# Down products in 64-column tiles, their sums over 128 rows, and coarser refills of four weight places

## What is computed

```python
def run_block(args):
    toks, wts, e = args
    xb = hf[toks]
    y = (jax.nn.silu(xb @ w_gate[e]) * (xb @ w_up[e])) @ w_down[e]
    return y * wts[:, None].astype(y.dtype)
...
out = jnp.zeros((N, D), h.dtype).at[slot_tok].add(ys.reshape(n_slots, D).astype(h.dtype))
```

## Time and profile before

| | |
|---|---|
| median of 3 runs | 1597.59 us (1597.54 to 1599.92) |
| profiled execution: its own time | 1597.35 us |
| profiled execution: span | 1595.5 us |
| PE busy over the span | 1570.9 us (98%) |
| DVE, ACT, POOL busy | 895.5, 192.5, 36.1 us |
| transfers | 374.70 MB, mean 235 GB/s |
| granted TensorE clock | 0.998 |
| chain that ended last | PE 88%, DMA 6%, SPq 3%, DVE 1% |

### The profile page before, as it was taken

How to read it: one execution, slowest core, us unless ns; L and a number is a source line. 1 busy time by engine, 2 the same in 40 slices (tenths; PEclk the granted TensorE clock), 3 DMA queues, 4 the chain that set the end, 5 groups by cost and what they waited for, 6 DMA issues and landing times.

```text
span 1595.5 us, 20636 instructions
## 1 busy us (share of the span) xinstructions
PE 1570.9 (98%) x8777; PEld 998.7 (63%) x8777; DVE 895.5 (56%) x1549; ACT 192.5 (12%) x311; POOL 36.1 (2%) x60
## 2 busy tenths in 40 slices
PE   8999999999999999999999999999999999999997
PEld 4866499974458564999744876899533333333332
DVE  5896676765559876676646676795432223121122
ACT  1321000000114110000001331410000000000001
POOL 1001000000010010000000000000000000000000
PEclk9999999999999999999999999999999999999999
DMA  6532545563534336355536333446999999999997
GB/s 212 205 106 106 177 149 164 169 215 107 211 96 171 106 106 210 120 160 180 189 106 237 131 107 132 159 161 256 424 383 427 426 426 429 427 426 427 427 422 302
DMA packets 129781, 374.70 MB, mean 235 GB/s; under 512 B 17220, under 2 KB 65672, under 8 KB 116632
## 3 DMA queue, kind: packets, MB, share of 16 engines
q1 hardware_dynamic: 118864, 370.62, 61.1%
q10 hardware_dynamic: 10824, 2.72, 0.8%
HBM read 372.28 MB, written 1.05 MB: 234 GB/s over the span
## 4 chain that ended last, share of the span: by engine, by line
PE 88%; DMA 6%; SPq 3%; DVE 1%; issue 0%; ACT 0%; POOL 0%; POOLq 0%; DVEq 0%
PE bank L892 16%; PE bank L1204 16%; PE bank L823 10%; PE bank L1648 10%; PE bank L835 6%; PE bank L1694 5%; PE bank L1457 4%; DMA weights<-in_w_down 4%; SPq L703 3%; DMA arena<-in_w_up 3%; PE bank L1407 3%; PE bank L1329 2%; PE bank L1187 2%; PE bank L1490 2%; PE bank L1339 2%; PE bank L843 2%
## 5 line engine op out<-in xcount | busy, mean ns | idle before, releaser
L823 PE MATMUL bank<-weights,turned_rows 128*128 128x512 f32 x384 | 169.6, 598 | 0.4 <-DVE turned_rows L2167 0.4
L3314 DVE TENSOR_TENSOR bc<-mix,bank 128x512 f32<-128x512 f32 x16 | 17.2, 1077 | 212.6 <-PE bank L1648 212.6
L892 PE MATMUL bank<-arena 128*128 128x512 f32 x296 | 133.2, 592 | 0.0
L823 PEld LDWEIGHTS bank<-weights,turned_rows 128*128 128x128 f32 x384 | 72.7, 192 | 86.5 <-issue 85.9
L1204 PE MATMUL bank<-arena 128*128 128x128 f32 x960 | 110.5, 275 | 0.0
L1204 PEld LDWEIGHTS bank<-arena 128*128 128x128 f32 x960 | 108.8, 192 | 0.0
L892 PEld LDWEIGHTS bank<-arena 128*128 128x128 f32 x296 | 56.0, 190 | 69.9 <-issue 67.9
L835 PE MATMUL bank<-turned_rows,weights 128*128 128x256 f32 x448 | 98.6, 380 | 0.0
L1648 PE MATMUL bank<-arena,mix 128*64 128x512 f32 x304 | 92.3, 595 | 1.1 <-DMA arena<-in_w_up 0.6
L835 PEld LDWEIGHTS bank<-turned_rows,weights 128*128 128x128 f32 x448 | 84.6, 190 | 12.1 <-issue 0.7
L1694 PE MATMUL bank<-arena,mix 128*32 128x512 f32 x512 | 86.3, 594 | 2.5 <-DMA weights<-in_w_down 1.4
(11 more groups left out here) (542 smaller groups left out, 2490.4 us busy)
## 6 DMA issues: line engine op xcount, KB each, us to landing
weights<-in_w_in SPq DMA_DIRECT2D x28, 2048.0 KB, 7.9
arena<-in_w_gate SPq DMA_DIRECT2D x13, 2048.0 KB, 22.7
arena<-in_w_up SPq DMA_DIRECT2D x12, 2048.0 KB, 34.0
weights<-in_w_ffn_gate SPq DMA_DIRECT2D x22, 1024.0 KB, 5.4
weights<-in_w_ffn_up SPq DMA_DIRECT2D x22, 1024.0 KB, 8.1
weights<-in_w_ffn_down SPq DMA_DIRECT2D x10, 2048.0 KB, 7.8
arena<-in_w_down SPq DMA_DIRECT2D x10, 2048.0 KB, 29.7
weights<-in_w_out SPq DMA_DIRECT2D x8, 2048.0 KB, 8.3
```

Source lines behind the costliest of these rows:

```text
L823: ins = mm(b[:, :], xT[:, k, t0 + P * t:t0 + P * t + P], w[:, k, :], start=(k == 0), stop=(k == KD - 1))
L892: ins = mm(b[:, :], lhs[:, j, :], rhs[:, j, :], start=(first and j == 0), stop=(last and j == pairs - 1))
```

## The change

Pairs 0 to 13 get wide forms of four steps; pairs 14 and 15 keep the old ones. `wide_down` issues two products per k and half, one for each expert, in 64-column tiles, and leaves the places ordered expert, row tile, place. Then the places of a row tile no longer lie in one half of the partitions. So `wide_sum_up` multiplies all 128 rows, with weights that are zero for the places of the other row tile; there is such a weight matrix for each row tile, hence `wide_pick_weights` (the same four small operations, into two 128 x 128 matrices that are cleared once), `wide_picks_turned` (two transposes) and `wide_picks_back` (a copy of 256 columns). Places 1, 2 and 3 are refilled in halves.

```diff
-REFILL_PARTS = (4, 4, 4, 4, 4, 4, 2, 2)
+REFILL_PARTS = (2, 2, 2, 2, 4, 4, 2, 2)
...
+            def wide_sum_up(n):
+
+                for half in range(2):
+                    pe.wait_ge(sem(f"y_ready{half}"), n + 1)
+                pe.wait_ge(sem("pickT_ready"), n + 1)
+                for half in range(2):
+                    for t in range(NT):
+                        mm(moe_bank[4 + 2 * t + half][:, :], wide_pickT[:, P * t:P * t + P], yE[:, 512 * half:512 * half + 512],
+                           start=(n == 0), stop=True, skip_group_check=True)
...
+            def wide_picks_turned(n):
+
+                pe.wait_ge(sem("pickw_ready"), n + 1)
+                for t in range(NT):
+                    ins = nc.tensor.transpose(moe_bank[1][:, P * t:P * t + P], wide_pickw_rows[t], ident[:, :])
+                ins.then_inc(sem("pickT_full"), 1)
+
+            def wide_down(w, half, k):
+
+                for e in range(2):
+                    at = TILE_COLS * e
+                    ins = mm(moe_bank[2 + half][at:at + TILE_COLS, :], hidT[:, k, at:at + TILE_COLS], w[e](2 * k + half),
+                             start=(k == 0), stop=(k == KE - 1), skip_group_check=True)
+                return ins
...
                 if n > 1:
-                    sum_up(n - 2, n == 2)
+                    wide_sum_up(n - 2)
                 expand(n, 2, 1, half_ready, all_ready).then_inc(sem("up_full"), 1)
...
-                rows_down(n_)
+                wide_rows_down(n_)
...
-                picks_turned(n_)
+                wide_picks_turned(n_)
                 next_rows(n_)
...
+            def wide_picks_back(n):
+
+                v.wait_ge(sem("pickT_full"), n + 1)
+                nc.vector.tensor_copy(wide_pickT, moe_bank[1][:, 0:NT * P]).then_inc(sem("pickT_ready"), 1)
...
-            pick_weights(0, 0, None)
+            nc.vector.memset(bc[:, 256:256 + NT * P], 0.0).then_inc(sem("dve_step"), 1)
+            step()
+            wide_pick_weights(0)
```

More of the change, by code:

```diff
@@ L410, in program @@
         pickw = pickw_rows.rearrange("p (t e j) -> p e t j", e=2, t=NT)
-        pickT = bc[:, 384:512]
+        wide_pickw_rows = [bc[:, 256 + P * t:256 + P * t + P] for t in range(NT)]
+        wide_pickw = [v.rearrange("p (e t j) -> p e t j", e=2, t=NT) for v in wide_pickw_rows]
+        wide_pickT = wrt.rearrange("p k n -> p (k n)")[:, 0:NT * P]
+        pickT = wide_pickT[:, 0:P]
         hidE = bc[:, NBC2:NBC2 + DE]
@@ L1699, in down_weights, with wide_rows_down @@
                 return [landed(n, 4 + e) for e in range(2)]
-            def rows_down(n):
+            def wide_rows_down(n):
                 w = down_weights(n)
-                if isinstance(n, int) and n == 0:
+                if n == 0:
                     for k in range(KE):
                         for half in range(2):
-                            ins = down(n, w, half, k)
+                            ins = wide_down(w, half, k)
                             if k == KE - 1:
@@ L1712, in rows_down @@
                     return
+                for half in range(2):
+                    for k in range(KE):
+                        ins = wide_down(w, half, k)
+                    ins.then_inc(sem("y_full"), 1)
+            def rows_down(n):
+                w = down_weights(n)
                 for half in range(2):
@@ L3293, in pick_weights, with wide_pick_weights @@
                 ins.then_inc(sem("pickw_ready"), 1)
+            def wide_pick_weights(n):
+                if n:
+                    v.wait_ge(sem("pickT_full"), n)
+                for t in range(NT):
+                    for e in range(2):
+                        r_ = rank[:, t, n * 2 + e:n * 2 + e + 1]
+                        g_ = gate[:, t, n * 2 + e:n * 2 + e + 1]
+                        ins = TS(wide_pickw[t][:, e, t, :], place, r_, g_, ALU.is_equal, ALU.mult)
+                ins.then_inc(sem("pickw_ready"), 1)
             def rows_in(n, xs=xsE[1]):
@@ L3350, in _ @@
                 hidden_back(i + 1, bank=2 if i == PAIRS - 3 else 0)
-                picks_back(i)
+                wide_picks_back(i)
                 if i < PAIRS - 4:
@@ L3355, in _ @@
                     rows_in(PAIRS - 1)
-                pick_weights(i + 1, i + 1, i + 1)
+                if i < PAIRS - 3:
+                    wide_pick_weights(i + 1)
+                else:
+                    pick_weights(i + 1, i + 1, i + 1)
                 if i % 2 and i + 4 < PAIRS:
```

## The result

| | before | after |
|---|---|---|
| median of 4 runs each | 1597.92 us | 1612.02 us (1611.34 to 1612.46) |
| ratio, 95% interval | | 1.0082 [1.0069, 1.0096] |
| profiled execution: span | 1595.5 us | 1610.4 us |
| chain that ended last | PE 88%, DMA 6%, SPq 3% | PE 98%, DMA 0% |

The change makes the kernel 14 us slower, 0.8%. The forecast was 1613.7 us. The spans of the two profiled executions differ by 14.9 us, the medians by 14.1.

A forecast was written before the change was run, and what follows sets the result against it. TensorE and transfers were taken as nearly level in the expert stage, TensorE bounding it after the change. Span 1595.5 + 22.7 (sums) + 0.1 (transpose) - 6.7 (waits) = 1611.6 us, with 1.85 and 0.24 added 1613.7 us; range 1607 to 1618.5.

The forecast's parts named there:

- What bounds the kernel: Expert stage: TensorE and transfers both look full; PE's 6.7 us of waits for transfers is its whole slack.
- Sums: Pairs 0 to 13: eight full-array records one after another, 1.62 us more per pair, 22.7 us in all, bounds 19.9 and 23.9.
- Waits that vanish: Expert stage from 1414 us on: all 6.7 us of PE's waits for transfers vanish, and TensorE bounds it to the end.
- Down products: Down products in 64-column tiles: same shape as gate and up, term 0.0, at most 0.4 us gained.
- Second transpose, wide copy, clearing: Pairs 0 to 13: transpose fits into the 0.21 us wait before the gather, copy and clearing cost nothing; 0.1 us in all.
- Refills: Places 1, 2 and 3 in halves: taken as 0, between 2.5 us earlier and 3.4 us later.
- Sum: Whole kernel: span 1595.5 + 22.7 + 0.1 - 6.7 = 1611.6 us, median 1613.7 us, 1.0% slower.
- Rival B: Wide sums are covered and transfers stay the bound: not slower, 1595.1 to 1601.0 us; chance 0.07.
- Rival C: Weight loads no longer hide in the wide sums: 1.5 us more per sum, 21 us in all, 1635 us; chance 0.04.
- Rival D: Second transpose and wide copy come to the path in 14 pairs: 4.8 us more, 1618.5 us; chance 0.09.
- Rival E: Cheaper: late transfers still make PE wait, or tiling changes cost nothing; 1610.8 us or less, to some 1606; chance 0.08.

## Why the prediction was right, step by step

**What bounds the kernel.** Right. In the kernel before TensorE and the transfers of weights finish within a few microseconds of each other, and the pool of PE's waits is what separates them. Shown by the flat and the steep part of the wide pairs, and by the refills in one piece, which cost the one kernel and not the other.

**Sums: 1.62 us more each, 22.7 in all.** The mechanism is right, the size is the upper bound that I had named: 1.71 each, 14 x 1.71 = 23.9. This is one of the two terms that were mis-sized and offset each other. The changes of tiling cost the full 0.29 of the row tiles, not 0.20. The step into the full array is 0.10 us longer, as taken; but so is the one from the first record to the second (1206.89 - 1206.36 = 0.53 in the timeline above, where the load of 1206.89 begins with the second record; the later steps are 0.43), and I had not counted it.

**Waits that vanish: 6.7 us.** All vanished, and more. From the chains of the version with narrow down products, 16.1 = 23.9 + 0.1 - x gives x = 7.9. Eight wide pairs give the same on their own: 8 x 1.56 + 0.16 - 4.60 = 8.0, where 1.56 is the growth of the period and the 0.16 takes back the gain of pair 0's down products, which stand ahead of the gate of pair 2. The medians (4.7 us, interval 2.7 to 6.1) bear it out less sharply. So the step that took the sum of the view of waits, 6.7, as the whole slack was 1.2 us short. That view counts from the modelled end of the product before, and unhindered products start before that end: in the earlier trace rows the first up product starts at 1208.74, the sums end at 1206.82 + 1.99 = 1208.81. At a wait it starts behind that end:

```profile
1501.31 1.99 PE L1659 MATMUL bank<-bc 64*128 64x512 f32 x8
...
1503.94 1.51 PE L1648 MATMUL bank<-arena,mix 128*64 128x512 f32 x6 [0.64 <-DMA arena<-in_w_up]
```

The view says 0.64, and the product is 0.71 later than it would be. Two more gaps, of 0.08 us each, at 1563.8 and 1573.9, are not in the view at all. With twelve waits, 12 x 0.07 + 0.16 = 1.0 us is my estimate of what the view leaves out, near the 1.2.

**Down products: 0.0.** Wrong by a term: 1.3 us were given back. I had taken the 7.02 of gate and up for 16 products of this shape. But a plain step is 0.43 us, and 16 of them are 6.9. The other 0.15 of the 7.02 is the change between tilings with which gate and up begin. In the order up, down the 64-column tiles of the one are followed by those of the other, so this change falls away, and the down piece is 6.87. Where a residual product over the full array stands between them it is 7.02 (1438.50 in the chain above). The version with 32-column tiles still pays for a change (7.00). A pair takes 1227.13 - 1199.53 = 27.60 us there and 27.44 here, 0.16 less. It is saved in the pairs where nothing stands between up and down, 0 to 8, of which 1 to 8 lie in the stretch that was measured: 8 x 0.16 = 1.3.

**Second transpose, wide copy, clearing.** Right: covered, 0.1 us in all, which is what the two transposes of pair 13, with no gather behind them, take over one (0.22 against 0.11 in the chains).

**Refills: 0.** Right in size, and for the reason given, later starts against larger transfers.

**Sum.** Forecast 22.7 + 0.1 - 6.7 = 16.1 us of span; measured 14.9. With the measured terms it is 23.9 + 0.1 - 7.9 - 1.3 = 14.8, the difference of the chains. This closes by construction, since the 7.9 was solved from them; what is independent is the 8.0 of the eight wide pairs. The errors of the first two terms (+1.2 and -1.2) cancel, which is luck: nothing ties the cost of a change between tilings to what the view of waits leaves out. What is left is the term of the down products.

**Rival B** (covered, no change) needed a sum dearer by 0.48 us at most; it is 1.71. The version with row-tiled sums, which leaves out half of each sum and measured 1597.46, shows how B would have looked. **Rival C** fell with the weight loads: they stay hidden in the wide sums too. The Trainium skill (TensorE: Matmul & The Clock Gate, The mechanism) has loads overlap products only where the row group differs, and names the background weight buffer as a second way to run ahead. In this trace loads of 0.19 us begin every 0.43 us under products with all 128 rows in use, so the first rule does not hold here; no run shows whether the buffer is the reason. **Rival D** fell with the transpose that fits into the wait, and with the wide copy that ends 1.2 us before it is needed. **Rival E** was right that the slack is more than the waits show, but the sums took the full 1.71 and the transfers were not waited for: 1612.02 is above its 1610.8.

No version here beats the kernel before. The row-tiled sums show why: 64-column down products make TensorE faster by 1.3 us where transfers set the end, and the ratio of 0.9995 [0.9986, 1.0004] shows no gain.

## What to carry to other kernels

A product over the full array with half of its rows zero costs as much as a full one: a step of 0.43 us here and in the earlier trace rows. Two row tiles at once are a factor of nearly two that a change of layout can lose without any product being added: here the sums stayed four products and went from 1.92 to 3.63 us.

Where two resources are nearly level, add up the waits of the one for the other over the whole stage, and treat the total as one pool. Work up to that total, standing ahead of the waits, was free (four wide pairs), and beyond it cost its full price (eight, fourteen). The total in the view of waits is a lower bound: it said 6.7 where 7.9 were there. A pair of experiments on either side of the crossover, and an edit to the other resource on both kernels, shows the bound better than any share of busy time.

## What the runs showed of the hardware that I had not expected

A change between tilings lengthens more than the step at the change: going into the full array, the first step and the one behind it are each 0.10 us over the plain 0.43, and the way there and back costs 0.29 us in all, the same as for row tiles. Down products in 32-column tiles behind up products in 64-column tiles cost 0.13 us more than in 64-column ones (7.00 against 6.87). The Trainium skill (TensorEngine Tiling (Array Packing), Key Properties) says that changing the tiling mode drains the TensorE. The longer steps here, 0.53 in place of 0.43 us, fit that; that a drain is their cause is not shown.

On VectorE a copy of 256 columns from a matmul bank took 0.41 us and one of 128 columns 0.28, so twice the columns cost 0.13 us more and not 0.28.
